# Routing of tile 0 and the samples ahead of the last output product, with part of tile 1's split on GpSimd

## The reference, cut to what matters

```python
x = x + merged @ w_out                                   # 264 x 1024, w_out 1024 x 1024
h = rmsnorm(x, norm_ffn)
logits = h @ w_router + b_router                         # 32 experts
top_vals, top_idx = top_k(logits, 4); gates = softmax(top_vals)
# for every token and each of its 4 experts e:
gate, up = split(h @ w_gate_up[e] + b_gate_up[e])        # 1024 x 2048 weights
gate = minimum(gate, 7); up = clip(up, -7, 7)
act = gate * sigmoid(1.702 * gate) * (up + 1)
y += gates[e] * (act @ w_down[e] + b_down[e])            # 1024 x 1024 weights
y = rmsnorm(x + y, norm_final)
```

## Time and profile before

| what | value |
|---|---|
| median of three runs | 1344.03 us (1339.4 to 1347.54) |
| profiled execution, its time | 1342.62 us |
| its span | 1340.8 us |
| mean granted TensorE clock | 0.991 |
| PE busy | 1275.6 us (95%) |
| DVE busy | 384.6 us (29%) |
| ACT busy | 228.1 us (17%) |
| POOL busy | 61.3 us (5%) |
| bytes moved by DMA | 516.96 MB, mean 386 GB/s |

### The profile page before, as it was taken

One profiled execution on the slowest core, in us unless ns is written; L12 is line 12 of the kernel. 1 busy time (PEld: TensorE's weight loads), 2 busy tenths in 40 slices (PEclk: granted clock), 3 DMA queues, 4 the chain that ended last, 5 costly groups with the idle time before them and its releaser, 6 DMA issues.

```text
span 1340.8 us, 18816 instructions
## 1 busy us (share of the span) xinstructions
PE 1275.6 (95%) x7701; PEld 635.6 (47%) x7701; DVE 384.6 (29%) x865; ACT 228.1 (17%) x369; POOL 61.3 (5%) x104
## 2 busy tenths in 40 slices
PE   6999999999979999999999999999999999999998
PEld 5675488787634343434434333334333333433334
DVE  3003865512244222222223222222222222222222
ACT  2011122302141111211111111111111111111112
POOL 2002514000000000000000000000000000000000
PEclk9999999999998999999999999999999999999999
DMA  9999987789965999999999999999999999999994
GB/s 334 386 338 322 354 315 270 272 291 324 413 237 233 422 428 429 427 428 429 429 428 427 429 430 428 429 428 428 430 428 429 428 428 429 428 429 428 429 429 198
DMA packets 57567, 516.96 MB, mean 386 GB/s; under 512 B 5615, under 2 KB 6855, under 8 KB 32160
## 3 DMA queue, kind: packets, MB, share of 16 engines
q1 hardware_dynamic: 50000, 493.68, 89.4%
q0 software_dynamic: 7344, 22.62, 5.1%
q10 hardware_dynamic: 192, 0.23, 0.1%
HBM read 512.98 MB, written 49.87 MB: 420 GB/s over the span
## 4 chain that ended last, share of the span: by engine, by line
PE 62%; DMA 30%; DVE 4%; issue 2%; ACT 1%; POOL 0%; SPq 0%; DVEq 0%; ACTq 0%; POOLq 0%
PE psum L585 59%; DMA weights<-in_w_gate_up 26%; PE psum L588 3%; DMA rel_copies<-rel_rows 2%; DVE spatial L1440 1%; DMA weights<-in_cache_mem_kv 1%; DMA weights<-in_w_mem_kv 1%; DVE late L1283 0%; DVE kvt L1026 0%; DVE x L1319 0%; DVE weights L1130 0%; DVE memory L1337 0%; DVE va L1151 0%; DVE va L1152 0%; ACT late L1593 0%
## 5 line engine op out<-in xcount | busy, mean ns | idle before, releaser
L585 PE MATMUL psum<-weights,spatial 128*64 128x512 f32 x1536 | 359.8, 601 | 19.0 <-DMA weights<-in_w_gate_up 17.7
L1409 DVE TENSOR_TENSOR hT<-psum,hT 128x264 f32<-128x264 f32 x256 | 92.9, 425 | 488.2 <-PE psum L585 488.2
L585 PE MATMUL psum<-weights,merged 128*64 128x512 f32 (+2 forms) x896 | 218.2, 595 | 0.0
L585 PEld LDWEIGHTS psum<-weights,spatial 128*64 128x64 f32 x1536 | 103.3, 137 | 212.7 <-issue 167.7
L585 PE MATMUL psum<-hT,weights 128*128 128x264 f32 x704 | 163.2, 389 | 1.8 <-DVE late L1283 0.9
L585 PEld LDWEIGHTS psum<-hT,weights 128*128 128x128 f32 x704 | 133.0, 191 | 28.8 <-DVE late L1283 5.1
L585 PEld LDWEIGHTS psum<-weights,merged 128*64 128x64 f32 (+2 forms) x896 | 72.2, 141 | 122.8 <-issue 120.9
L1649 ACT COPY bT<-psum 128x264 f32<-128x264 f32 x33 | 12.5, 379 | 474.4 <-PE psum L588 474.4
L1440 DVE TENSOR_SCALAR spatial<-psum,lowest 128x512 f32<-128x512 f32 x64 | 48.1, 751 | 148.9 <-PE psum L585 145.5
L585 PE MATMUL psum<-bT,merged 64*128 64x264 f32 x512 | 74.3, 409 | 0.0
L585 PEld LDWEIGHTS psum<-bT,merged 64*128 64x128 f32 x512 | 44.0, 186 | 55.6 <-issue 51.9
(11 more groups left out here) (286 smaller groups left out, 860.8 us busy)
## 6 DMA issues: line engine op xcount, KB each, us to landing
weights<-in_w_gate_up SPq DMA_DIRECT2D x96, 2048.0 KB, 32.4
weights<-in_w_down SPq DMA_DIRECT2D x48, 2048.0 KB, 34.0
memory<-in_w_gate_up SPq DMA_DIRECT2D x16, 2048.0 KB, 32.4
late<-in_w_gate_up SPq DMA_DIRECT2D x16, 2048.0 KB, 33.9
out<-in_cache_win_kv SPq DMA_DIRECT2D x8, 4094.0 KB, 23.3
weights<-in_w_in SPq DMA_DIRECT2D x13, 2048.0 KB, 16.2
late<-in_w_down SPq DMA_DIRECT2D x8, 2048.0 KB, 32.8
memory<-in_w_down SPq DMA_DIRECT2D x8, 2048.0 KB, 33.4
```

The source lines that it names most:

```text
L585: return nc.tensor.matmul(out, lhsT, rhs, start=start, stop=stop, **kw)
L1409: V.tensor_tensor(acc[:, c, :], p_a[j % 2][part], acc[:, c, :], ALU.add).then_inc(s_acc, 1)
```

## The change

The order of the last steps is new. Tile 0's and the samples' transposes, split and routing come around the product ("wo", 1, 0); the router product and the sum of its parts are cut into part 0 (tiles 0 and 2) and part 1 (tile 1); the top-eight search is done per part. Between the two parts stands the last output product, whose first two row blocks are emitted ahead of part 0's `lg`. For tile 1, GpSimd computes the scaled rows in h_tok and both subtractions, VectorE none. ScalarE takes the exponent ahead of tile 1's middle part. The down bias moves from GpSimd's queue to SyncE's, behind the eighth chunk. `count_over` moves ahead of the gate weights, and lgT is th[0] in place of a part of bT_all.

```diff
-    s += [("wos", 0), ("wos", 1), ("wo", 0, 0), ("woz", 0), ("wo", 0, 1), ("woz", 1), ("scale", 0), ("hi", 2), ("hi", 0)]
-    s += [("wo", 1, 0), ("xt", 2, 0), ("xt", 0, 0), ("rest", 2), ("wo", 1, 1), ("xt", 0, 1), ("xt", 1, 0), ("scale", 1), ("xt", 1, 1)]
-    s += [("rest", 0), ("hi", 1), ("lo", 2), ("lo", 0), ("rt",), ("rest", 1), ("lg",), ("top",), ("pos",)]
+    s += [("wos", 0), ("wos", 1), ("wo", 0, 0), ("woz", 0), ("wo", 0, 1), ("woz", 1), ("xt", 0, 0), ("xt", 0, 1), ("xt", 2, 0)]
+    s += [("scale", 0), ("hi", 2), ("hi", 0), ("rest", 2), ("rest", 0), ("wo", 1, 0), ("rt", 0), ("lo", 2), ("lo", 0), ("lg", 0), ("wo", 1, 1)]
+    s += [("xt", 1, 0), ("xt", 1, 1), ("scale", 1), ("rt", 1), ("hi", 1), ("lg", 1), ("top",), ("rest", 1), ("pos",)]
...
+            sp.wait_ge(s_yzero, 1)
+            sp.dma_start(y_upper[0:E, :], I["b_down"][0, :, 0:512]).then_inc(s_bdown, 16)
+            sp.dma_start(y_lower[0:E, :], I["b_down"][0, :, 512:1024]).then_inc(s_bdown, 16)
             experts(0, 0, RING)
...
-            pool.wait_ge(s_job, job[("rt",)] + 1)
+            pool.wait_ge(s_job, job[("wo", 1, 1)] + 1)
             nc.gpsimd.memset(y_tok, 0.0).then_inc(s_yzero, 1)
-            pool.wait_ge(s_yzero, 1)
-            pool.dma_start(y_upper[0:E, :], I["b_down"][0, :, 0:512]).then_inc(s_bdown, 16)
-            pool.dma_start(y_lower[0:E, :], I["b_down"][0, :, 512:1024]).then_inc(s_bdown, 16)
+            pool.wait_ge(s_scale, 2)
+            nc.gpsimd.tensor_scalar(h_tok, x1[:, 1, :], stat[:, 24 + NORMED[1]:25 + NORMED[1]], None, ALU.mult).then_inc(s_xnorm, 1)
+            pool.wait_ge(s_xnorm, 1)
+            pool.wait_ge(s_xhi, 3)
+            nc.gpsimd.tensor_tensor(h_tok, h_tok, xparts[:, 0, 1, :], ALU.subtract).then_inc(s_xrest, 1)
+            pool.wait_ge(s_xmid, 3)
+            nc.gpsimd.tensor_tensor(xparts[:, 2, 1, :], h_tok, xparts[:, 1, 1, :], ALU.subtract).then_inc(s_xlo, 1)
...
-                    last = row_tile(o, merged, weights(f"o{n}"), t, 512)
+                    last = row_tile(o, merged, weights(f"o{n}"), t, 512, range(2 if (t, n) == (1, 1) else 0, KD))
...
+                    taken(pe, *(("xt", 2, 0) if part == 0 else ("xt", 1, 0)))
+                    for seg, (t0, tn) in enumerate((TILES[0], TILES[2]) if part == 0 else (TILES[1],)):
+                        for k in range(KD):
+                            if k == 4:
+                                taken(pe, "xt", part, 1)
+                            r = slice(k % 4 * E, (k % 4 + 1) * E)
+                            last = mm(o[r, seg * P:seg * P + tn], wr[:, k, :], rowsT[:, k, t0:t0 + tn], k < 4, k >= 4)
...
+                    if part == 0:
+                        follower = job[("wo", 1, 1)]
+                        pe.wait_ge(s_taken[follower % 3], follower // 3)
+                        row_tile(bank[follower % 3], merged, weights("o1"), 1, 512, range(2))
+                    taken(pe, "rt", part)
+                    for t, at in ((0, 0), (2, P)) if part == 0 else ((1, P + NS),):
+                        tn = TILES[t][1]
+                        last = mm(o[0:tn, t * E:(t + 1) * E], lgT[:, at:at + tn], quarters)
...
+                    if t == 1:
+                        continue
...
+                elif kind == "rt" and a[0] == 0:
+                    ready()
+                    V.tensor_copy(lgT[:, 0:P + NS], o[:, 0:P + NS]).then_inc(free, 1)
...
                 if isinstance(b, int):
-                    low_part(1)
+                    count_over()
                     gate_weights()
                 take_x(b * (E + 1))
-                if isinstance(b, int):
-                    count_over()
...
-                    A.copy(xparts[0:tn, 1, t, :], x1[0:tn, t, :]).then_inc(s_xmid, 1)
-                elif kind == "rt":
+                    A.copy(xparts[0:tn, 1, t, :], h_tok if t == 1 else x1[0:tn, t, :]).then_inc(s_xmid, 1)
+                elif kind == "rt" and a[0] == 1:
                     act.wait_ge(s_job, n + 1)
-                    A.copy(lgT[:], o[:, 0:NT]).then_inc(free, 1)
+                    A.copy(lgT[:, P + NS:NT], o[:, 0:P]).then_inc(free, 1)
```

More of the change, by code:

```diff
@@ L602, in wide_tile, with row_tile @@
                 return last
-            def row_tile(out, lhs, w, t, n):
+            def row_tile(out, lhs, w, t, n, ks=range(KD)):
                 t0, tn = TILES[t]
-                for k in range(KD):
+                for k in ks:
                     last = mm(out[0:tn, 0:n], lhs[:, k, t0:t0 + tn], w[:, k, 0:n], k == 0, k == KD - 1)
@@ L850, in _ @@
                 elif kind == "rt":
+                    part, = a
                     pe.wait_ge(s_router, 1)
[L852 to L859, removed]
-                elif kind == "lg":
-                    taken(pe, "rt")
-                    for t, (t0, tn) in enumerate(TILES):
-                        last = mm(o[0:tn, t * E:(t + 1) * E], lgT[:, t0:t0 + tn], quarters)
+                    taken(pe, *(("xt", 2, 0) if part == 0 else ("xt", 1, 0)))
[5 more added lines that the diff above has]
+                            last = mm(o[r, seg * P:seg * P + tn], wr[:, k, :], rowsT[:, k, t0:t0 + tn], k < 4, k >= 4)
+                elif kind == "lg":
+                    part, = a
+                    if part == 0:
[6 more added lines that the diff above has]
+                        last = mm(o[0:tn, t * E:(t + 1) * E], lgT[:, at:at + tn], quarters)
                 elif kind == "pos":
@@ L1340, in _ @@
                         V.tensor_tensor(bias[2 * E:3 * E, 0:2 * D], brow, flat_qk.bitcast(BF16)[0:E, 0:2 * D], ALU.subtract).then_inc(s_bias, 1)
+                elif kind == "rt" and a[0] == 0:
+                    ready()
+                    V.tensor_copy(lgT[:, 0:P + NS], o[:, 0:P + NS]).then_inc(free, 1)
                 elif kind == "lg":
+                    part, = a
                     ready()
                     dve.wait_ge(s_grows_in, 16)
-                    dve.wait_ge(s_scale, 2)
-                    for t, (_, tn) in enumerate(TILES):
+                    dve.wait_ge(s_scale, part + 1)
+                    ts = (0, 2) if part == 0 else (1,)
+                    for t in ts:
+                        tn = TILES[t][1]
                         ins = V.scalar_tensor_tensor(lg[0:tn, t, :], o[0:tn, t * E:(t + 1) * E], stat[0:tn, 24 + NORMED[t]:25 + NORMED[t]],
                                                      br[0:tn, :], ALU.mult, ALU.add)
-                        if t < 2:
+                        if t != ts[-1]:
                             seq(ins)
@@ L1351, in _ @@
                     own()
-                elif kind == "top":
-                    for t in range(3):
+                    for t in ts:
                         seq(V.max(mx8[:, t, :], lg[:, t, :]))
                         seq(V.max_index(idx[:, t, :], mx8[:, t, :], lg[:, t, :]))
+                elif kind == "top":
                     seq(V.tensor_scalar(idf, idx[:], 1.0, None, ALU.add))
```

4 lines of the change are left out of this document (2 added, 2 removed).

## The result

| | before | after |
|---|---|---|
| median, 20 runs each | 1340.75 us (1338.27 to 1348.41) | 1347.71 us (1343.88 to 1353.94) |
| profiled execution | 1342.62 us | 1348.55 us |
| its span | 1340.8 us | 1346.8 us |
| mean granted TensorE clock | 0.991 | 0.991 |

The ratio of after to before is 1.0045, 95% interval 1.0034 to 1.0057, some 6.0 us (4.6 to 7.6); the two medians alone lie 6.96 us apart. I had forecast a gain of 2.8 us and gave 0.80 to a difference within 0.5%. The difference does lie within 0.5%, but the sign was wrong and the time is outside my range, by 0.2 us above its upper end. That it is so near is luck: the forecast stood on 1344.03, the median of three runs, and twenty give 1340.75. From there the forecast would have been 1338.0 and the upper end 1344.2.

A forecast was written before the change was run, and what follows sets the result against it. The end was taken to follow the ninth transfer, held by expert 0's start. Masks 2.4 us earlier plus 0.35 gave 2.8: 1344.0 - 2.8 = 1341.2 us, range 1336.5 to 1347.5.

The forecast's parts named there:

- What bounds the kernel: Transfers run full from 440 us on; a microsecond cut from the 15.8 us hole before the ninth transfer shortens the end equally.
- The work ahead of the last product: Waits, router part 0 (1.1 us) and the split last product put the last output add at 394.2, 2.6 us later.
- The chain behind the last add: From last output add to masks 6.1 us in place of 11.17; masks at 400.3, gate weights ready at 404.7.
- GpSimd's part, which must stay hidden: Tile 1's multiplication (1.1 us) and two subtractions (2.1 each) finish 0.55 us before TensorE wants the low part.
- my own fence: Bounds on GpSimd's 1024-element passes: 1.06 us from a memset's rate, 5.2 from a reduction over partitions.
- GpSimd is slow: Rival: GpSimd's subtractions at the reduction's rate delay the gather's last products; expert 0 at 411.7, median 1346.4 us; chance 0.12.
- d of 5.2: Time in us of one GpSimd subtraction at the reduction's rate; the forecast itself took 2.1, with loss from 4.0.
- The rival of blocking: GpSimd's subtractions hold up VectorE at mask comparison and gate weights; expert 0 0.4 us later, median 1344.4 us; chance 0.30.
- The gain of 2.8: Masks 2.4 us earlier plus 0.35 between masks and expert 0; ninth transfer at 411.8.
- The kept clock: Rival: closer work keeps TensorE's clock up through gather and expert 0's start; 4.9 us gained together, 1339.1 us; chance 0.10.

The follow-up runs named there:

- e1: The changed kernel plus one tiny unused GpSimd tensor_scalar of eight columns, ahead of GpSimd's wait for the last product; median 1341.22 us, ratio to before 0.9997.
- e7: The changed kernel plus a tiny GpSimd clear and product behind part 0's sum, ahead of the wait for the last product; 1341.57 us, one run.
- e3: The changed kernel with GpSimd's three arithmetic instructions undone, tile 1's split on VectorE, low part behind the gate weights; median 1342.98 us, ratio to before 1.0005.
- E0: Not a run: the start of expert 0's first row, 53.34 us behind the start of the samples' output product before, 58.58 after.
- e8: e3 plus 28 useless bfloat16 products of 512 columns in TensorE's empty stretches; median 1338.15 us, ratio to before 0.9981.
- e4: The kernel before plus a tiny unused GpSimd tensor_scalar behind its wait for the last product, ahead of the clear of y_tok; 1343.86 us, one run.
- e5: e3 with GpSimd's code loaded early and three useless two-input GpSimd passes over 128x1024 behind the scale; 1344.12 us, one run.
- e6: e3 with GpSimd's code loaded early and three useless one-input GpSimd passes over 128x1024 behind the scale; 1340.58 us, one run.
- e12: e3 with the down bias's two transfers back on GpSimd's queue, behind the clear of y_tok; 1343.52 us, one run.
- e2: e1 with the multiplication of tile 1's rows by the scale moved from GpSimd to VectorE; median 1340.37 us, ratio to before 0.9999.

## Why the prediction was wrong

**What bounds the kernel: right.** c9 sets the end to within 1.7 us in thirteen traces. I read the change at the right place.

**The work ahead of the last product: right.** The last add comes 2.14 later from T0 (forecast 2.6), router part 0 took 0.75 (forecast 1.1, lower bound 0.7).

**The chain behind the last add: right.** 5.92 against 6.1; the gate weights were ready at 403.35 against 404.7.

**"GpSimd's part, which must stay hidden": the step that failed.** I wrote that it waits for the scale and for the high part, and put the first subtraction at 398.5 to 400.6. Three things stood in it. First, what GpSimd does after its operands are there: nothing for 8.56 us, because its first ordinary arithmetic starts 10.5 us behind the configuration. That is the whole loss: with the load elsewhere (e1, e7) c9 is 6.6 to 6.8 us earlier, and the ratio of e1 is 0.9997. I had bounded each operation's price from two sides, and not the way from one operation to the next of another kind. The row that would have told me was in my own fence: the reduction with 10.28 of idle time in front of it, whose price I took as 0.81. Its releaser reads as TensorE there, and as "issue" in the trace of after (10.21). A first use of an engine's routine has to be read with the idle time ahead of it. Second, the multiplication, which I sized at 1.1 by a memset, took 2.85 (also in e1 and e7, loaded early), beyond the 1.7 up to which I had called it free. Third, the subtraction was sized right, 2.12 against 2.1.

**The rival "GpSimd is slow" had the right place and the wrong mechanism.** The gather's last products waited for GpSimd and expert 0 came late, as it said, at 413.64 against its 411.7. But its d of 5.2 is refuted by 2.12. My upper bound of the damage came from it, and so was too low.

**The rival of blocking was real and hidden.** It didn't cause this loss. Once the load is gone it takes back the gain: e1 and e3 differ by 0.18 us. What I held against it was misread: the clear at 394.98 overlaps the subtraction that ends at 395.02 by 0.04 us, and a clear reads nothing, so it could say little either way. Had the stall not existed, the measured result would have been near 0.9997, within my "same", for a reason to which I gave 0.30 and not for the one I forecast.

**The gain of 2.8 was not reached in any kernel without added products.** e3 and e1 have 0.9 and 0.7 at c9. In e3, the low part stays on VectorE and binds the gather; in e1, blocking does. Whether the rest of the 2.8 is there is not shown: that needs the new order with a GpSimd that costs VectorE nothing, and no run has it.

**The kept clock** I gave 0.10, as an effect of closer work. It did not come by itself: 0.54 from 398.8 to 420 after. Brought about by the added products of e8 it is worth 2.15, near the 2.1 that I had computed: 0.2 at E0 (I had said 0.5) and 1.95 in the first 16 products (1.6).

The spread of T0, 8 us from work ahead of the change, makes single times of this kernel blind to a step of 1 us; e4, e5, e6, e7 and e12, with one time each, are judged by their distances from T0. What sets T0 stays open.

## What to carry to other kernels

Before giving an engine its first work of a new kind near the critical path, look in the trace for its earlier first uses and read the idle time in front of them, above all where the releaser is "issue" behind a configuration instruction; then put a tiny instruction of that kind behind its last idle place. Work moved from VectorE to GpSimd need not be time saved on VectorE while both touch SBUF (here 2.5 us moved, 3.3 us came back as blocking): price it by the instruction of VectorE that will stand beside it. Where a stage border leaves TensorE nearly empty and at the lower clock, products that nobody reads, put in the gap, can be worth more than a shorter chain; here they made the difference between no gain and 0.2%.

## What the runs showed of the hardware

- GpSimd: 7.9 to 10.5 us between its configuration instructions and the first ordinary arithmetic behind them (after, e1, e2, e5, e6, e7), and 9.0 to 10.7 ahead of a partition reduction. The configuration is issued behind the preceding GpSimd instruction, not at the wait in the code (e4: 235.3, for an instruction at 391.68). The clear of y_tok and issuing transfers paid nothing.
- GpSimd over 128x1024 float32: 2.12 with two inputs, 2.85 for a multiplication by a scalar per partition, 2.77 to 3.17 by an immediate (e6). One input was slower than two, which took 1.89 to 2.09 in e5.
- VectorE beside a two-input GpSimd pass: two-input instructions of 0.26 took 2.00 and 1.78 (e1), a one-input one of 0.18 took 1.98 (e2). Beside a one-input pass: two-input 0.56 as always (e1, e7), one-input of 0.18 took 1.01 (e6), 0.86 (e7) or 0.18 (e1).
- TensorE's granted clock stayed 1.00 over a stretch where it was 0.50 (404 to 412 us in e3 and e8), when 28 products of 512 columns filled its gaps.
